# A two-layer decoder trunk on one Trainium2 core: the second layer's gate and up in groups of seven block products, and the last product's weight sums grown by transfers

## What is computed

```
x = x + y @ w_out[l]
h = rms_norm(x, ffn_norm_w[l])
x = x + (jax.nn.silu(h @ w_gate[l]) * (h @ w_up[l])) @ w_down[l]
return rms_norm(x, final_norm_w)
```

## Time and profile before

| | |
|---|---|
| median of three runs | 1218.61 us |
| the profiled execution, its own time | 1218.75 us |
| its span | 1216.9 us |
| PE busy | 1201.6 us, 99% |
| DVE busy | 784.4 us, 64% |
| ACT busy | 566.3 us, 47% |
| granted PE clock, mean | 0.997 |

### The profile page before, as it was taken

The page is one execution under the profiler, slowest core; times in us unless marked ns, Lnnn a source line. Parts: engine busy times, 40 slices in busy tenths (PEclk is TensorE's granted clock), DMA queues, the critical chain, the costliest instruction groups (busy, mean ns, idle before and its releaser), DMA issues.

```text
span 1216.9 us, 16112 instructions
## 1 busy us (share of the span) xinstructions
PE 1201.6 (99%) x5831; PEld 972.4 (80%) x5831; DVE 784.4 (64%) x1233; ACT 566.3 (47%) x917; POOL 107.1 (9%) x209
## 2 busy tenths in 40 slices
PE   9999999999999999999999999999999999999998
PEld 7876648888888878888888788788888888888876
DVE  6787886786667763337677666545665455456796
ACT  6354455655555543325585254444243232324564
POOL 0000000011110100000002814400000000000120
PEclk9999999999999999999999999999999999999999
DMA  6243311687867533331322211022244443336881
GB/s 247 90 118 91 106 54 52 225 189 174 210 174 187 108 100 91 100 104 55 119 87 70 87 35 53 18 61 66 83 134 116 116 109 104 93 104 223 167 147 70
DMA packets 56643, 138.04 MB, mean 113 GB/s; under 512 B 21890, under 2 KB 22146, under 8 KB 56322
## 3 DMA queue, kind: packets, MB, share of 16 engines
q1 hardware_dynamic: 48754, 111.44, 28.7%
q0 software_dynamic: 6912, 24.38, 11.4%
q10 hardware_dynamic: 912, 1.35, 0.4%
HBM read 128.61 MB, written 2.10 MB: 107 GB/s over the span
## 4 chain that ended last, share of the span: by engine, by line
PE 89%; DVE 5%; ACT 3%; issue 1%; DMA 1%; ACTq 0%; SPq 0%; DVEq 0%
PE PS L2168 87%; PE PS L2481 1%; DVE wring L1648 1%; DMA raw<-w_stream 1%; PE PS L2244 1%; DVE resid L1652 0%; DVE kept L1688 0%; DVE cacc L1843 0%; ACT wring L924 0%; ACTq L1194 0%; DVE wring L1698 0%; PE PS L2559 0%; DVE AA L1692 0%; DVE out L2159 0%; DVE amax L1761 0%
## 5 line engine op out<-in xcount | busy, mean ns | idle before, releaser
L2168 PE MATMUL PS<-HH,wring 128*128 128x512 f32 x2136 | 506.2, 393 | 0.9 <-DVE vd L2094 0.9
L2168 PEld LDWEIGHTS PS<-HH,wring 128*128 128x128 f32 x2136 | 395.2, 188 | 81.4 <-issue 1.3
L2168 PE MATMUL PS<-wring,HH 128*128 128x512 f32 x672 | 156.0, 390 | 0.3 <-ACT wring L1139 0.3
L2168 PEld LDWEIGHTS PS<-wring,HH 128*128 128x128 f32 x672 | 125.7, 188 | 26.6 <-issue 0.6
L1698 DVE TENSOR_TENSOR wring<-raw,wring 128x1024 fp32r<-128x1024 f32 x91 | 111.8, 1231 | 48.2 <-ACT wring L924 48.1
L924 ACT ACTIVATE wring<-raw 128x1024 fp32r<-128x1024 f32 x91 | 95.8, 1056 | 96.0 <-PE PS L2168 68.6
L2168 PE MATMUL PS<-AS,wring 128*128 128x512 f32 x528 | 120.4, 389 | 0.0
L2168 PEld LDWEIGHTS PS<-AS,wring 128*128 128x128 f32 x528 | 99.0, 188 | 20.5
L2168 PE MATMUL PS<-wring,AA 128*128 128x512 f32 x462 | 105.4, 389 | 1.6 <-DVE wring L1648 0.8
L2168 PEld LDWEIGHTS PS<-wring,AA 128*128 128x128 f32 x462 | 86.6, 188 | 20.3 <-issue 2.3
L1464 DVE TENSOR_TENSOR ubuf<-PS,rstd 128x512 f32<-128x512 f32 x22 | 15.2, 690 | 83.9 <-PE PS L2168 83.9
(11 more groups left out here) (367 smaller groups left out, 1606.1 us busy)
## 6 DMA issues: line engine op xcount, KB each, us to landing
raw<-w_stream SPq DMA_DIRECT2D x131, 512.0 KB, 3.5
x_even<-w_glu POOLq DMA_DIRECT2D x12, 512.0 KB, 6.3
raw<-w_glu SPq DMA_DIRECT2D x10, 512.0 KB, 9.4
y_part<-w_glu SPq DMA_DIRECT2D x10, 512.0 KB, 6.6
w_part<-w_glu SPq DMA_DIRECT2D x10, 512.0 KB, 5.3
w_part<-w_glu POOLq DMA_DIRECT2D x10, 512.0 KB, 10.9
kept<-w_last POOLq DMA_DIRECT2D x10, 512.0 KB, 8.3
x_odd<-w_glu POOLq DMA_DIRECT2D x8, 512.0 KB, 6.2
```

Of the source, the lines that this page charges most:

```text
L2168: return nc.tensor.matmul(out, lhsT, rhs, start=start, stop=stop, skip_group_check=adds)
```

## The change

Layer 2 now does what layer 1 does: four plain tiles, then five groups of seven block products, with functions that take the layer as an argument (`ffn_gated`, `load_group`, `grow_group`, `glu_products(l, j)`). `x_part` has one buffer in both layers, so its load for group j+1 waits until ACT and DVE have split tiles 12 and 13 of group j, and it stands at the end of group j in SP's program. The 16 residual transfers stand together behind the first group's loads; DVE's eight transposes of the residual stand between its splits of tiles 4 to 7 of that group. In the last product the order is P_12, P_11, P_21, P_22, P_SUM, P_LAST, P_ALL, all four weight sums are made by POOL's accumulating transfers, and differences of the left side that were made while gate and up ran are made in the groups (`halves`) or in the last product (`cross`). The last group's results are turned inside P_12, ahead of its fourth piece. In layer 1's `down` the turning is moved behind two chunks of columns 0 and 1, and of 2 and 3.

```
-T_DN1 = T_GU1 + 2 * KF
+T_DN1 = T_GU1 + PLAIN + GROUPED * GLU_STEPS
-P_12, P_11, P_22, P_21, P_SUM, P_ALL, P_LAST = range(PRODUCTS)
+P_12, P_11, P_21, P_22, P_SUM, P_LAST, P_ALL = range(PRODUCTS)
...
+        def load_group(l, j):
+
+            if j == 0:
+                load_part(l, x_part, 0, j, 0, 0)
+            for p in range(2):
+                t = glu_tile(l, j, G_M12, p)
+                before = raw_before(t)
+                sp.wait_ge(hi_ready[before % RING], slot_round(before))
+                sp.wait_ge(lo_ready[before % RING], slot_round(before))
+                sp.dma_start(raw[:, t % RAW], glu_d[l, j, 0, 1][:, p * TILE:(p + 1) * TILE]).then_inc(raw_loaded[t % RAW], 16)
+            load_part(l, y_part, 2, j, 1, 1)
+            load_part(l, w_part, 4, j, 1, 0)
+            if j + 1 < GROUPED:
+                load_part(l, x_part, 0, j + 1, 0, 0)
...
-            if t >= RESIDUAL_AFTER and (t - RESIDUAL_AFTER) % 2 == 0 and (t - RESIDUAL_AFTER) // 2 < 16:
-                residual_blocks((t - RESIDUAL_AFTER) // 2)
+        sp.wait_ge(tile_used, T_GU1)
+        for j in range(GROUPED):
+            load_group(1, j)
+            if j == 0:
+                for m in range(16):
+                    residual_blocks(m)
...
-        for a, part, behind in ((P_21, B21, P_11), (P_LAST, B21, P_21), (P_ALL, B12, P_SUM)):
+        for a, part, behind in ((P_21, B21, P_11), (P_SUM, B22, P_21), (P_LAST, B21, P_22), (P_ALL, B12, P_SUM)):
             for i in range(PIECES):
-                add_to_kept(a, i, part, behind)
+                add_to_last(a, i, part, behind)
...
+                if g == 4:
+                    keep_turned(1, GROUPED - 1, 0)
+                    left_high(P_12, 4)
+                    keep_turned(1, GROUPED - 1, 2)
+                    left_high(P_12, 5)
+                    keep_turned(1, GROUPED - 1, 1)
+                    keep_turned(1, GROUPED - 1, 3)
...
+            elif l and 4 <= step < 8:
+                for n in (2 * step - 8, 2 * step - 7):
+                    turn_residual(n)
...
-                if g // PIECES == P_21:
-                    i = g % PIECES
-                    dve.wait_ge(first_loaded[i // 3], 32)
-                    dve.wait_ge(lo_ready[last_tile(g) % RING], slot_round(last_tile(g)))
-                    V.tensor_tensor(kept_tile(i), kept_tile(i), more_tile(i), ALU.add).then_inc(sem("lhs_made"), 1)
+                if g == 4:
+                    halves(9)
+                    halves(10)
+                    left_low(P_12, 4)
+                    left_low(P_12, 5)
+                if a == P_22:
+                    cross(P_LAST, i)
+                if g < 36:
+                    left_low(a + 1, i)
+                if a == P_SUM:
+                    cross(P_ALL, i)
...
-        gate_up(T_GU1, E_GU1, 3)
+        plain_gate_up(1, T_GU1, E_GU1)
+        for j in range(GROUPED):
+            glu_products(1, j)
...
+                if a == P_12 and i == 3:
+                    pe.wait_ge(sem("ffn_mul"), glu_made(1, GROUPED - 1, "up_second", 1))
+                    turn_results(1, GROUPED - 1, (0, 2, 1, 3), LAST_TURN_BANK)
...
+            columns(0, (0, 1))
+            turn_results(0, end, (0, 1), TURN_BANK)
+            columns(0, (2, 3))
+            pe.wait_ge(sem("ffn_mul"), glu_made(0, end, "up_second", 1))
+            columns(2, (0, 1))
+            turn_results(0, end, (2, 3), TURN_BANK)
+            columns(2, (2, 3))
```

More of the change, by code:

```diff
@@ L35 @@
 T_GU0 = T_OUT0 + KD
[L36 removed]
+PLAIN = 4
 GROUPED = 5
@@ L71 @@
 B11, B12, B21, B22 = (0, 0), (0, 1), (1, 0), (1, 1)
-P_12, P_11, P_22, P_21, P_SUM, P_ALL, P_LAST = range(PRODUCTS)
[L73 to L76, removed]
+P_12, P_11, P_21, P_22, P_SUM, P_LAST, P_ALL = range(PRODUCTS)
+OUT_ORDER = (0, 1, 2, 3)
+PRODUCT_BANK = (4, 0, 4, 0, 2, 0, 4)
+CONTINUED = (P_21, P_22, P_LAST, P_ALL)
+ON_KEPT = (P_11, P_21, P_SUM, P_ALL)
+ADDED = (P_21, P_SUM, P_LAST, P_ALL)
 ADDING = 3
@@ L605, in raw_count @@
     def raw_count(t):
[L607 to L611, removed]
+        return 16 * sum(uses_raw(u) for u in range(t % RAW, t + 1, RAW))
     def raw_tile(t):
@@ new lines, in keep_turned, with gate_first_silu @@
+        def keep_turned(l, j, c):
+            ending = l and j == GROUPED - 1
+            act.wait_ge(sem("glu_turned"), 4 * (GROUPED * l + j) + (c + 1 if not ending else (0, 2, 1, 3).index(c) + 1))
+            bank = (LAST_TURN_BANK if ending else TURN_BANK)[c]
+            nc.scalar.activation(kept_chunk(2 + 4 * j + c), PS[:, bank], ACT.Copy).then_inc(sem("glu_kept"), 1)
+        def gate_first_silu(l, j):
+            for b in range(2):
+                act.wait_ge(sem("ffn_mul"), glu_made(l, j, "gate_first", b))
+                nc.scalar.activation(gate_first[:, b], gate_first[:, b], ACT.Silu, scale=rtok[:, b:b + 1]).then_inc(sem("gate_silu"), 1)
@@ L1577, in ffn_first, with cross, ffn_gated @@
+        def cross(a, i):
+            dve.wait_ge(sem("halves_made"), 2 * HALF)
+            of = P_22 if a == P_LAST else P_21
+            dve.wait_ge(sem("ffn_lo"), split_count(of, i))
+            start, stop = rows_of(i)
+            V.tensor_tensor(full_left(a, i), full_left(a, i), pfull[:, start:stop], ALU.subtract).then_inc(sem("halves_made"), 1)
+        def ffn_gated(l, tg, eg):
+            made = SPLITS[l]
+            left_sums(l)
+            dve.wait_ge(sem("ffn_hi"), made + 1)
             V.scalar_tensor_tensor(left_minus[:, :, 1], scaled[:, 4:8], -1.0, left_minus[:, :, 0].bitcast(f32), ALU.mult, ALU.subtract).then_inc(sem("ffn_lo"), 1)
-            dve.wait_ge(sem("ffn_hi"), 2)
+            dve.wait_ge(sem("ffn_hi"), made + 2)
@@ L1666, in after_product @@
[L1666 to L1671 removed]
+                    dve.wait_ge(sem("last_sums"), b + 1)
@@ L2126, in _ @@
         out_proj(3, T_OUT1, E_OUT1)
-        norm_finish(3, 7)
-        for n in range(KD):
-            V.transpose(turned[:, :, n], xT[:, n].rearrange("p (t c) -> p t c", c=P)).then_inc(sem("resid_turned"), 1)
-        ffn_last(T_GU1, E_GU1)
+        ffn_gated(1, T_GU1, E_GU1)
         last_product()
```

848 lines of the change are left out of this document (417 added, 431 removed).

## The result

| | before | changed |
|---|---|---|
| median of 20 runs each | 1217.76 us (1217.31 to 1219.77) | 1220.72 us (1218.52 to 1223.05) |
| profiled execution: own time, span | 1218.75, 1216.9 us | 1222.74, 1221.0 us |
| PE busy | 1201.6 us, 99% | 1187.2 us, 97% |

The ratio is 1.0023, 95% interval 1.0016 to 1.0029: slower by 3.0 us, where 1215.2 was forecast. The time lies inside the range of 1202 to 1222; the likeliest case was a small gain, and the slower side had 0.17.

A forecast was written before the change was run, and what follows sets the result against it. PE was taken to bound the kernel, busy 1201.6 of 1216.9 us. Terms: 1218.75 - 18.5 - 1.5 - 1.55 + 1.9 + 1.2 + 13.4 + 1.7 = 1215.4, 1215.2 for the median; range 1202 to 1222.

The forecast's parts named there:

- the fourth sum, last product: Last product: a transfer takes over DVE's fourth weight sum, so PE's two 0.8 us gaps go, -1.55 us.
- M21 in group 0: Layer 2, group 0: DVE's eight residual transposes ahead of `glu_q` delay the bank PE wants, +1.9 us.
- P_12's piece 4: Last product: turning inside P_12 and two `halves` on DVE delay piece 4's low half, +1.2 us.
- M12 of group 1: Layer 2, group 1: PE waits for M12's first tile, queued behind 16 residual transfers, +13.4 us (bounds 2.5 and 20.2).
- the clock behind it: After the long wait ahead of group 1's M12, PE's granted clock falls for a while, +1.7 us.
- The rival of the pace of issue: Residual transfers flow as fast as SP issues them, 0.6 us each; M12 wait 2.5 us, total 1202.7; chance 0.25.
- No wait at all: Layer 2, group 1: the ring's four tiles cover the residual transfers, PE never waits, total 1200.2; chance 0.05.
- 16b + 2a - 6.65: M12 wait in us; b is the price of a residual transfer (0.94), a of an accumulating one (2.5).
- The landing time that I had named as the sign of b: M12 tile's load in group 1: about 14 us if forecast holds, 4 at pace of issue, over 20 if starved.
- One buffer for `x_part`: Group ends, both layers: some 4 us left for the load; if it or P_21's tiles miss, 1220.2; chance 0.08.
- The starved group's case: Layer 2, group 1: residual transfers cost 1.3 us, accumulating ones 3.0; wait 20.2, total 1222.0; chance 0.17.
- the forecast's case: Layer 2, group 1: a residual transfer costs 0.7 to 1.2 us of the full engines; chance 0.45.

The follow-up runs named there:

- experiment 8: Changed kernel, residual transfers split six behind group 0's `w_part`, ten behind group 1's; `gate_first` a tile earlier, low halves first, last four transposes behind `glu_q`: 1197.52 us.
- experiment 6: Kernel before the change with only `down`'s new order, twelve products ahead of each turning: 1216.06 us beside 1217.84.
- experiments 1: Changed kernel with all 16 residual transfers moved from ahead of layer 2 group 1's `raw` tiles to behind its `w_part`: 1204.88 us.
- experiment 2: Changed kernel with eight residual transfers left ahead of group 1's `raw` tiles and eight moved behind its `w_part`: 1212.6 us.
- experiment 5: Changed kernel with `gate_first` behind the split of tile 0 and `up_second` behind that of tile 2, each one tile earlier on DVE: 1215.95 us.
- Experiment 4: Changed kernel with DVE making `gate_first` of the group before behind the split of tile 0 in place of tile 1: 1218.09 us.
- experiment 7: Changed kernel, DVE's residual transposes behind the splits of tiles 8 to 11 of group 0, and P_12's low halves 4 and 5 ahead of two `halves`: 1219.91 us.
- experiment 3: Changed kernel with POOL's accumulating transfers of layer 2's group 1 held until all 16 residual transfers have landed: 1214.07 us.
- 10: Changed kernel with each residual transfer as 128 rows of 1024 bytes over 128 partitions, blocks in wrong places: 1214.43 us.
- 11: Changed kernel with each residual transfer as 32 rows of 4096 bytes read from HBM, leaving the residual out: 1214.7 us.

## Why the prediction was wrong, step by step

Each term, forecast and measured in the profiled executions, from the start of one row to the start of the next (so a gap counts some 0.2 to 0.3 us more than the idle time that its row shows):

| step | forecast | measured |
|---|---|---|
| 120 products less, 80 transposes | -18.5 | -18.2 |
| layer 1's `down` | -1.5 | -1.7 |
| the fourth sum, last product | -1.55 | -1.9 |
| M21 in group 0 | +1.9 | +1.9 |
| P_12's piece 4 | +1.2 | +1.5 |
| M12 of group 1 | +13.4 | +16.5 |
| the clock behind it | +1.7 | +3.0 |
| M11 of layer 1's groups | 0 | +2.1 |
| M11 of layer 2's groups | 0 | +1.2 |

The measured column sums to +4.4, the medians differ by 3.0, the spans by 4.1. The products: layer 2 without gaps is 221.3 us (23.64 to group 0, 38.1, four times 39.9), 19.9 less than the 241.2 of before, and the 16 transposes in P_12 give 1.7 back. Piece 4 is the last product's 108.2 us (1107.03 to 1215.2) less the 106.7 of experiment 8, which has no gap there; the fourth sum is 106.7 less those 1.7, less the 107.0 of before. The profiled execution also started 1.1 us later, and between 784 and 788 its clock did not fall as it had before, 1.4 us less; neither is the change's.

**Steps that held.** The products, `down` (experiment 6 alone), the fourth sum (no gap in P_22 and P_SUM, 66 products in 15.1 us each; no run tells it from the new order of the products), the two small DVE gaps at their places and sizes. (Two slips in the sums changed nothing: M21's 265.6 less 263.6 is 2.0, and 5.5 low halves of 0.68 are 3.7 us.) That the M12 tile cannot pass the 16 transfers held too (experiments 1 and 2); the Trainium skill's rule that each engine takes a ring's descriptors in order ("DMA: Bandwidth & Descriptors", section "Queues, rings and completion order") agrees with both, though the tile was not even issued before the 16, so the order within a ring was not put to the test. The rival of the pace of issue fell: 0.86 us each, not 0.6. "No wait at all" fell.

**Steps that failed.** *The M12 wait* was not mis-sized by its prices. With the measured b = 0.86 and a = 2.8 the formula 16b + 2a - 6.65 gives 12.7. What it lacks is the end of the wait: I let PE start when the tile is split, and it needs an empty bank as well, 3.4 us later. 12.7 + 3.4 = 16.1, against the 16.3 of the row; experiment 5 took 2.7 of it away. I had costed the results on DVE at nothing because they cost nothing in layer 1, where the tile before them is never late. They are chained to tiles, and when the tile is late so are they. The landing time that I had named as the sign of b misled as well: with SP held at the issue, the M12 tile landed 4.9 us after it, the first rival's "4", behind a wait of 16.3. The lateness was in the time of the issue, 938.49.

*One buffer for `x_part`.* I had given the late load a chance of 0.08 on "some 4 us left". The load was indeed in time for the tile, but not for `gate_first`, which stood behind the split of its second half: 0.1 to 0.7 us a group (in layer 2: 0.3 ahead of group 1, where 886.75 to 927.03 is 40.28 for 38.1 and M21's 1.9, 0.2 in its M11, then 0.13, 0.47 and 0.14), together 3.3. Gaps in layer 1's groups were a sign of being wrong that the prediction had named. Experiment 4 gave 2.6 back by moving one line.

*The clock.* I took 1.7 us from two slices in another part of the program. The fall came, but the term was too small: the 24 products behind the wait took 8.57 us against 5.60, 3.0 us more where I had put 1.7. The kernel before has no wait of such a length to read this from.

On the base of 1217.76 the forecast is 1214.4; the errors of these terms add 3.1 + 1.3 + 2.1 + 1.2 = 7.7, those of the others cancel, which gives 1222.1. The median is 1.4 below that; the profiled execution, from which the terms are read, was itself 2.0 over its median. The starved group's case, at 1222.0, had the right size for the wrong reason: with 0.86 and 2.8 us the queue was near the forecast's case, and the rest came from the banks and the clock. That the time lies inside the range is to that extent luck.

## What to carry to other kernels

When transfers are moved in a queue, count the bytes and the engines' rate as well as the issues, and look for the air in front of a load that waits anyway: the same 16 transfers cost 19 us of PE in one place and about 1 spread over two others. Follow a wait to everything that PE needs at that instruction, the bank as well as the tile, and put the work that empties a bank ahead of the work of a tile that may be late. A gap of 3.0 us cost 2.9 more in the clock (experiment 7) and one of 16.3 us 3.0 more, so by these rows one long wait is cheaper than several short ones.

## What the runs showed of the hardware

A transfer within the buffer of 128 KB, as 1024 rows of 128 bytes, took 0.86 us in the mean of 16 with a tile's load ahead of them, and 0.74 us at the 178 GB/s of full engines in their midst (experiment 3); a tile of 512 KB that adds to its place took 2.8 by the difference of two runs, where the earlier trace rows have a plain tile at 1.25 to 1.5. While POOL's two ran, one issue on SP lasted up to 3.7 us (0.70 in the median): SP's queue was held while the engines were behind.

The granted clock fell to its lower level (1.2 GHz) in or behind waits of 3.0, 4.4, 13.2 and 16.3 us, and the 24 products behind them took 8.51, 7.75, 7.95 and 8.57 us instead of 5.60. It fell in the seven other waits of these runs between 9.5 and 16.9 us too, with 7.08 (experiment 2, a wait of 9.9) to 8.36 us. After waits of 1.6 and 1.35 us they took 5.75 and 5.74, about what they took after gaps of 0.3. So the price of the clock was 1.5 to 3.0 us and did not follow the length of the wait. Between 784 and 788 us the clock fell in the profiled executions of the kernel before and of experiments 1, 3, 7, 10 and 11, and not in that of the changed kernel or of the other experiments, at the same work. The changed kernel's stage, against the earlier trace rows:

```profile
784.00:786.00 2.00, 1.86 (x18) 1.56 (x18) 1.36 (x4) 0.95 (x3) 0.00 (x0) 1.00 0.00 0
```

Such a fall cost 1.4 us, by the stretch from `down` to layer 2. The kernel before shows its like between its own executions: those with a mean granted clock of 0.997 took 1218.4 to 1219.3 us, most of those with 0.999 or 1.0 took 1217.0 to 1218.3.
